# Scattering routed rows while projecting: one region per expert in place of gathers and accumulating scatters

## The reference, cut to what matters

```
proj = x @ w_in                       # 5 blocks of 512 columns
m    = concat(conv_mixer(proj), rg_lru(proj) * gelu(gate)) @ w_out
x    = layer_norm(ALPHA * x + m, ln1)
# routing: best of 4 groups, then the best 2 of its 4 experts
gates  = softmax(top-2 expert logits) * softmax(group logits)[group]
h = silu(x @ w1[e]) * (x @ w3[e])     # 16 experts, 1024 -> 256
y = sum over the row's 2 experts of (h * gate) @ w2[e]
out  = layer_norm(ALPHA * x + y, ln2)
```

## Time and profile before

| | us |
|---|---|
| median of three runs | 1322.22 (1317.29 to 1328.05) |
| profiled execution, first to last instruction | 1314.2 |
| TensorE busy in it | 1132.7 (86%) |
| VectorE busy | 710.5 (54%) |
| ScalarE busy | 522.3 (40%) |
| GpSimd busy | 298.0 (23%) |

### The profile page before, as it was taken

The page is one execution under the profiler, slowest core; times in us unless marked ns, Lnnn a source line. Parts: engine busy times, 40 slices in busy tenths (PEclk is TensorE's granted clock), DMA queues, the critical chain, the costliest instruction groups (busy, mean ns, idle before and its releaser), DMA issues. The chain is left out here.

```text
span 1314.2 us, 19578 instructions
## 1 busy us (share of the span) xinstructions
PE 1132.7 (86%) x5748; PEld 1021.3 (78%) x5749; DVE 710.5 (54%) x1131; ACT 522.3 (40%) x678; POOL 298.0 (23%) x254
## 2 busy tenths in 40 slices
PE   6999999999999999999999269999999899996000
PEld 6999999999999998888887157877787778885000
DVE  5676544644555564434334755555646445531698
ACT  4554533634445453333333204444445434421222
POOL 1000000000000021121211242345535443432244
PEclk9999999999999999999999559999999999999555
DMA  5422100200120155544432535787888877764822
GB/s 181 137 85 74 56 19 19 97 19 19 35 88 13 52 166 190 173 144 160 144 128 100 205 112 179 212 279 200 267 224 233 257 194 207 206 125 62 324 112 100
DMA packets 64423, 183.95 MB, mean 140 GB/s; under 512 B 7456, under 2 KB 34096, under 8 KB 60176
## 3 DMA queue, kind: packets, MB, share of 16 engines
q1 hardware_dynamic: 42464, 104.28, 22.4%
q0 software_dynamic: 17040, 61.57, 19.1%
q10 hardware_dynamic: 4896, 17.83, 3.3%
HBM read 125.70 MB, written 57.96 MB: 140 GB/s over the span
## 5 line engine op out<-in xcount | busy, mean ns | idle before, releaser
L1296 PE MATMUL ps_h<-w_hi,xt_hi 128*128 x336 | 136.5, 406 | 0.0
L1296 PE MATMUL ps_h<-w_hi,xt_lo 128*128 x336 | 132.8, 395 | 0.0
L1296 PE MATMUL ps_h<-w_lo,xt_hi 128*128 x336 | 132.8, 395 | 0.0
L272 PE MATMUL ps_vb_c<-x_hi,w_hi 128*128 (+1 forms) x320 | 114.0, 356 | 10.7 <-DVE x_lo L424 10.7
L272 PE MATMUL ps_vb_c<-x_lo,w_hi 128*128 (+1 forms) x320 | 113.2, 354 | 0.0
L272 PE MATMUL ps_vb_c<-x_hi,w_lo 128*128 (+1 forms) x320 | 113.1, 353 | 0.0
L272 PE MATMUL ps_va_b<-x_hi,w_hi 128*128 (+1 forms) x320 | 112.3, 351 | 0.0
L272 PE MATMUL ps_va_b<-x_hi,w_lo 128*128 (+1 forms) x320 | 112.1, 350 | 0.0
L272 PE MATMUL ps_va_b<-x_lo,w_hi 128*128 (+1 forms) x320 | 111.9, 350 | 0.0
L1246 POOL DMA_INDIRECT acc_scr<-out_sb,id_s x42 | 76.2, 1813 | 35.4 <-POOL id_s L1242 27.9
L193 POOL DMA_DIRECT2D w_raw<-in_w_in x15 | 8.0, 531 | 328.8 <-DVE w_lo L410 320.4
(11 more groups left out here) (246 smaller groups left out, 2722.3 us busy)
## 6 DMA issues: line engine op xcount, KB each, us to landing
w_raw<-in_w SPq DMA_DIRECT2D x16, 2048.0 KB, 8.6
w_raw<-in_w SPq DMA_DIRECT2D x16, 1024.0 KB, 9.2
w_raw<-in_w_in POOLq DMA_DIRECT2D x19, 512.0 KB, 3.7
w_hi_p<-in_x_rows SPq DMA_DIRECT2D x17, 512.0 KB, 3.8
x_scr<-w_lo_p ACTq DMA_DIRECT2D x17, 512.0 KB, 2.6
acc_scr<-w_lo_p ACTq DMA_DIRECT2D x17, 512.0 KB, 2.6
v<-acc_scr SPq DMA_DIRECT2D x17, 512.0 KB, 10.5
x_raw<-in_x_t SPq DMA_DIRECT2D x20, 416.0 KB, 3.5
```

The source lines that it names most:

```text
L272: mm = pe.matmul(ps[i][:, 0:CHUNK], w[:, i, k], x[:, k, bass.ds(c * CHUNK, CHUNK)], start=(k == 0 and n == 0), stop=(k == KT - 1 and n == 2))
L1296: mm = pe.matmul(ps_h[par][:], x[:, par, k], w[:, bass.ds(at, 1), k].rearrange("p o n -> p (o n)"), start=(k == 0 and n == 0), stop=(k == ...
```

## The change

`x1_scr` and `acc_scr` go. In their place are `xs_scr`, a region of CAP = 2080 rows for each of the 16 experts, `g_scr`, a gate for each of these rows, and `o_scr`, an output row for each slot of the 48 steps.

- **Zeroing.** After the first channel group of the mixer, SyncE writes zeros over the first 128 rows of each region, the gates of these, and the last 15 tiles of `o_scr` (`FEWEST` = 33 to 48), from a source 256 elements wide that is read four times.
- **Projection.** Row tiles lie in a ring of eight. The norm is two VectorE operations; the sum with beta on GpSimd and the stores of `x1` and ALPHA * `x1` go. TensorE's order is: six of the eight k-slices of tile t, transposes of t-1, a count for a pair of tiles, the last two k-slices, the router of t-1. For each pair of tiles VectorE routes (`assign`: groups, experts, one-hot; `places`: the row's place in its expert's region, with a running count), and GpSimd scatters each row tile twice into `xs_scr` and its gates twice into `g_scr`. The last two tiles (group `LAST`) are routed after the stage.
- **Before the experts.** `plan_steps` makes the list of steps: expert, first row in `xs_scr`, whether weights are split. `slots` turns places into rows of `o_scr` for the end. An expert's last tile begins early enough to be full (it overlaps the one before) where the expert has over 128 rows.
- **Experts.** SyncE loads the rows and the gates of step s+3 with plain transfers, after it has stored the output of step s-1, also plain. ScalarE keeps ALPHA/2 times the row tile, and VectorE adds it to the output when it leaves PSUM (`evict`, both halves). The weights are now loaded through GpSimd's queue.
- **Last stage.** GpSimd gathers each row's two output rows, VectorE adds them, and does the norm, gain and beta in two operations.

`assign` is 21 operations on 128 x 8 to 128 x 32 elements and `places` 14, nearly all of which wait for the one before; `free` in `load(s)` is s - 3.

The diff, cut to its core:

```diff
@@ mixer: mix_sync
         store_y(0, NCH - 1, True)
+        sp.wait_ge(s_zero, 1)
+        for e in range(NE):
+            sp.dma_start(xs_scr[e * CAP:e * CAP + P, :].rearrange("p (a d) -> p a d", d=ZC),
+                         zero.unsqueeze(1).broadcast_to((P, D // ZC, ZC))).then_inc(s_zo, 16)
+            sp.dma_start(g_scr[e * CAP:e * CAP + P, :], zero[:, 0:1]).then_inc(s_zo, 16)
+        for n in range(FEWEST, STEPS):
+            sp.dma_start(o_scr[n * P:n * P + P, :].rearrange("p (a d) -> p a d", d=ZC),
+                         zero.unsqueeze(1).broadcast_to((P, D // ZC, ZC))).then_inc(s_zo, 16)
         with sp.Fori(1, GROUPS - 1) as j:
             with sp.Fori(0, NCH - 1) as c:
                 store_y(j, c, False)
@@ class Router
+    def assign(self, dve, n):
...
+    def counts(self, pe, n, bank, before, ones):
+        pe.wait_ge(self.s_asg, n + 1)
...
+        pe.matmul(bank[:, 0:m * NE], before, rhs, start=True, stop=True)
+        pe.matmul(bank[:, 2 * NE:(2 + m) * NE], ones, rhs, start=True, stop=True).then_inc(self.s_cnt, 1)
+    def places(self, dve, n, bank):
...
+    def scatter(self, pool, n):
+        pool.wait_ge(self.s_sl, n + 1)
+        for t, rows, c in todo:
+            pool.indirect_dma_start(self.xs_scr, bass.IndirectOffsetOnAxis(self.sli[0:rows, t, c:c + 1], 0),
+                                    self.ring[t % NRING][0:rows], None).then_inc(self.s_sc[n % 4], 16)
+        pool.wait_ge(self.s_wts, n + 1)
+        for t, rows, c in todo:
+            pool.indirect_dma_start(self.g_scr, bass.IndirectOffsetOnAxis(self.sli[0:rows, t, c:c + 1], 0),
+                                    self.wts[0:rows, t, c:c + 1], None).then_inc(self.s_gs, 16)
@@ mix_project_phase: TensorE
+            for t in range(NT):
+                project(t, early)
+                if t >= 1:
+                    turn(t - 1)
+                for n in ends_at(t - 2):
+                    rt.counts(pe, n, ps_c, before, ones)
+                project(t, late)
+                if t >= 1:
+                    route(t - 1)
@@ mix_project_phase: VectorE, after residual, statistics and low half of y
+                dve.scalar_tensor_tensor(out=v, in0=v, scalar=mv[:, par, 0:1], in1=ln_g,
+                                         op0=ALU.subtract, op1=ALU.mult).then_inc(s_xn, 1)
...
+                dve.scalar_tensor_tensor(out=v, in0=v, scalar=rstd[:, par:par + 1], in1=ln_b,
+                                         op0=ALU.mult, op1=ALU.add).then_inc(s_x1, 1)
+                for n in ends_at(t - 2):
+                    rt.places(dve, n, ps_c)
+                if t >= 1:
+                    logits_out(t - 1)
+                for n in ends_at(t - 1):
+                    rt.assign(dve, n)
@@ moe_phase: SyncE
+            def load(s, par, h):
+                row = sp.value_load(plan[0:1, 1, bass.ds(s, 1)], min_val=0, max_val=NE * CAP - P)
...
+                if not early(s, 2):
+                    sp.wait_ge(s_xr, read)
+                    sp.wait_ge(s_tx, read)
+                    sp.wait_ge(s_g[par], there)
+                sp.dma_start(xg[:, par], xs_scr[bass.ds(row, P), :]).then_inc(s_xg[par], 16)
+                if not early(s, XS):
+                    sp.wait_ge(s_ev, free)
+                sp.dma_start(gate[:, slot(par, h)], g_scr[bass.ds(row, P), :]).then_inc(s_g[par], 16)
+            def store(s, par):
+                sp.wait_ge(s_ev, s + 1)
+                sp.dma_start(o_scr[bass.ds(s * P, P), :], out[:, par]).then_inc(s_st[par], 16)
+            def step(s, par, h, left):
+                if not early(s, 1):
+                    store(s - 1, 1 - par)
+                if left == 2:
+                    load(s + 3, 1 - par, h + 1 + par)
+            sp.wait_ge(s_plan, 1)
+            for n in range(LAST - 3, LAST + 1):
+                sp.wait_ge(rt.s_sc[n % 4], rt.landed(n))
+            sp.wait_ge(rt.s_gs, 16 * TOPK * NT)
@@ moe_phase: GpSimd
+            pool.dma_start(ew.w13_raw[:], w13[0]).then_inc(ew.s_r13, 16)
+            pool.dma_start(ew.w2_raw[:], w2[0]).then_inc(ew.s_r2, 16)
+            for n in (LAST - 1, LAST):
+                rt.scatter(pool, n)
...
+            with pool.Fori(2, NE) as e:
+                pool.wait_ge(s_13lo, e * 2)
+                pool.dma_start(ew.w13_raw[:], w13[bass.ds(e, 1)].rearrange("o p k n -> p (o k) n")).then_inc(ew.s_r13, 16)
+                pool.wait_ge(s_2lo, e)
+                pool.dma_start(ew.w2_raw[:], w2[bass.ds(e, 1)].rearrange("o p k n -> p (o k) n")).then_inc(ew.s_r2, 16)
@@ moe_phase: ScalarE, after x_hi(s + 1) and ahead of the weight split
+                act.activation(flat(xr[:, slot(par, h)]), xg[:, par], ACT.Copy, scale=ALPHA / 2).then_inc(s_xr, 1)
@@ moe_phase: VectorE, in place of the copy of half the output
+            def evict(s, par, h):
+                dve.wait_ge(s_o, s + 1)
+                dve.wait_ge(s_xr, s + 1)
...
+                for f in range(2):
+                    ins = dve.tensor_tensor(out[:, par, c], ps_o[f][:], flat(xr[:, slot(par, h), c]), ALU.add)
+                ins.then_inc(s_ev, 1)
@@ finish_phase: GpSimd
+            for t in range(NT):
+                for c, to in enumerate((v, v1)):
+                    pool.indirect_dma_start(to[0:n, t], None, o_scr,
+                                            bass.IndirectOffsetOnAxis(sfin[0:n, c, t:t + 1], 0)).then_inc(s_in[t], 16)
```

More of the change, by code:

```diff
@@ new lines, in landed, with mix_project_phase, sb, sem @@
+    def landed(self, n):
+        return 16 * TOPK * sum(GROUPED[i][1] for i in range(n % 4, n + 1, 4))
+def mix_project_phase(nc, x_t, w_in, w_lru, chan, y_scr, states, x_rows, w_out, w_router, ln, consts_in,
+                      xs_scr, g_scr, o_scr, logits, small, wreg, x_raw, rt):
+    with ExitStack() as ctx:
+        mx = mixer(nc, ctx, x_t, w_in, w_lru, w_out, chan, y_scr, states, x_rows, wreg, x_raw, xs_scr, g_scr, o_scr)
+        mix_sync, mix_gpsimd, mix_tensor, mix_scalar, mix_vector = mx.engines
+        STEPS_MIX = GROUPS * NCH
+        LAST = len(GROUPED) - 1
+        def sb(name, shape, dt=F32):
+            return ctx.enter_context(nc.sbuf_tensor(name, shape, dt))
+        def sem(name):
+            return ctx.enter_context(nc.semaphore(name))
+        squares, wr, ring = mx.squares, mx.wr, mx.ring
+        ident, before, ones = (squares[:, i] for i in range(3))
@@ L931, in lo2, with moe_phase @@
                           ALU.subtract).then_inc(self.s_2lo, 1)
-def route_phase(nc, consts, logits, ids, gates, plan, ew, w13, w2, ln, ln2, consts_in, small):
+def moe_phase(nc, rt, xs_scr, g_scr, o_scr, w13, w2, ln, consts_in, wreg, sfin):
     with ExitStack() as ctx:
@@ L1172, in experts_phase @@
+        xr, xg, out = rows(wreg[2], 0, XS), rows(wreg[3], 0, 2), rows(wreg[3], 2, 4)
+        gate = sb("gate", [P, XS])
+        consts = sb("consts_sb", [P, NCONST])
+        plan = sb("plan", [1, 3, STEPS + 2], I32)
         xt_hi = sb("xt_hi", [P, 2, KT, P], F32R)
@@ L1249, in step @@
-            def step(s, par, h, left):
-                if left == 2:
-                    gather(s + 3, 1 - par)
-                if not early(s, 1):
-                    add(s - 1, 1 - par)
-            for s in range(3):
-                gather(s, s % 2)
-            last = steps(pool, step)
-            add(last, 1)
-            pool.wait_ge(s_xg[0], last * 8 + 24)
-            pool.wait_ge(s_add, last * 16 + 16)
+            pool.dma_start(ew.w13_raw[:], w13[0]).then_inc(ew.s_r13, 16)
+            pool.dma_start(ew.w2_raw[:], w2[0]).then_inc(ew.s_r2, 16)
@@ L1304, in step @@
                 mm.then_inc(s_th, 1)
+            pe.wait_ge(s_con, 16)
+            rt.counts(pe, LAST, ps_c, consts[:, C_TRI:C_TRI + P], consts[:, C_ONE:C_ONE + P])
+            pe.wait_ge(s_vals, 1)
+            pe.wait_ge(rt.s_read, LAST + 1)
+            for i in range(3):
+                mm = pe.matmul(ps_c[0:1, 128 + i * (STEPS + 1):128 + (i + 1) * (STEPS + 1)], vals[:, i:i + 1],
+                               consts[:, C_ID:C_ID + STEPS + 1], start=True, stop=True)
+            mm.then_inc(s_pp, 1)
             turn(0, 0, 0)
-            last = steps(pe, step)
+            last, _ = steps(pe, step)
             output(last, pe.value_load(plan[0:1, 0, bass.ds(last, 1)], min_val=0, max_val=NE - 1))
@@ L1348, in step, with then @@
                 act.wait_ge(s_sil, s + 1)
+            rt.gate_exp(act, LAST)
+            ew.hi13(act, 0, first)
+            ew.hi2(act, 0, first)
             x_hi(0, 0)
-            last = steps(act, step)
+            residual(0, 0, 0)
+            last, _ = steps(act, step)
             h_hi(last)
-            out_half(last, 1)
         @block.vector
         def _(dve):
+            def then(ins):
+                rt.then(dve, ins)
             def h_lo(s):
@@ L1394, in _, with finish_phase @@
+            rt.assign(dve, LAST)
+            rt.places(dve, LAST, ps_c)
+            dve.wait_ge(s_con, 16)
+            plan_steps()
+            ew.lo13(dve, 0, first)
```

(8 more changed lines are left out.)

808 lines of the change are left out of this document (356 added, 452 removed).

## The result

The changed kernel takes 1502.6 us in the median of four runs (1499.8 to 1504.0), against 1323.9 (1317.3 to 1328.1, four runs, three of which were known ahead of the prediction) before: a ratio of 1.137, 95% interval 1.133 to 1.141. Forecast were 1339 us and a range of 1296 to 1363. The direction was the likeliest one of the forecast, the size was not in it. The profiled execution has a span of 1500.7 us; before it was 1314.2, so 186.5 us have to be found.

The account below looks back on a forecast made before the run. TensorE was taken to bound mixer, projection and expert steps, VectorE the routing tables and last stage. Terms +15 + 6 - 26 + 24.5 - 2 = +17.5 gave span 1331.7, median 1339.7, stated as 1339 us, range 1296 to 1363.

Parts of the forecast that it names:

- The direction: Whole kernel: slower than 1335 us, given 0.48, against 0.28 for faster than 1309 and 0.24 for within.
- Mixer, +15: Mixer: zeroing on SyncE's queue delays a y store, so TensorE idles 15 us once (9 to 25).
- Small columns that cost more: Mixer zeroing: 4-byte gate columns, named only as part of what could take the 15 us wait up to 25.
- Rival 5: Mixer: the zeroing does not hold it up, -15 us on any other case; no chance of its own.
- Projection, +6: Projection: count matmuls about 0.4 us a pair plus stalls, norm covered; together +6 us (0 to 16).
- The stall at the counts: Projection: TensorE waits 0 to 1 us for the pair's routing at the count matmuls, in eight pairs.
- To the experts, -26: Last projected tile to first expert matmul: 45 us instead of 71.1, saving 26 (20 to 31).
- Expert steps, +24.5: Expert steps: base 403.5 us, plus loads 3 us late in 14 steps, 42 us; 445.5 in all (-17.5 to +52.5).
- rival 3: Expert steps: weights go first, whole; loads 5 us late, 70 us, total 1367; 0.14, shared with forecast plus rival 4.
- Tail and last stage, -2: After the last expert matmul: tail gains 5.8 us, VectorE-bound last stage loses 3.9; -2 (-4 to +20).
- Rival 4: Last stage: GpSimd's gathers become the limit, 99 us instead of 89, +8 to +17; 0.14 with the forecast, shared with rival 3.

Follow-up runs that it names:

- e1: Changed kernel with the sixteen 4-byte gate columns of zeros written as one transfer of 16 rows of 512 bytes; 1420.7 us.
- e9: e8 with tile 16's y split moved behind the pair's routing on VectorE and the x1_t eviction on ScalarE; 1287.5 us, ratio to before 0.974.
- e8: Changed kernel plus e1, all zeroing spread over y stores, expert loads before stores, e6, tile 16's y split after tile 14's norm; 1295.3 us, ratio to before 0.978.
- e6: Changed kernel with the first two row loads not waiting for gate scatters, and expert 1's weights issued only after these loads land; 1493.7 us.
- e11: e9 with expert weights in six transfers of 4 KB per partition, and expert 0's weights on SyncE's queue; 1299.0 us, ratio to before 0.982.
- e4: Changed kernel with each expert's weights in six transfers of 4 KB per partition instead of two of 16 and 8 KB; 1435.9 us.

## Why the prediction was wrong, point by point

**Mixer, +15: measured +100.9. This step failed, in one term.** The row blocks were priced at 46 us and cost 44.5 (e1), TensorE's wait for them at 15 and was 15.9. "Small columns that cost more" had no term of their own in the sum, only a share of the 10 us up to the end of the range; beside the row blocks they cost 82. No row of before shows 4-byte writes side by side, so the bound was a guess, and it should have been much wider: sixteen transfers that nothing in the trace resembles stood ahead of a store that TensorE waits for. Rival 5 (-15) was wrong too.

**Projection, +6: measured +26.0.** Some 10 us of it is tile 14's round trip for the last tile's y (251.0 becomes 240.3 in e9, 10.0 of it in the pitch of the next tile; 8.7 are shown by the one move from e8 to e9). The order on VectorE there was in the code and I did not follow it. The rest, 15.3 us, is in e9 a pitch of 14.6 us in seven tiles with counts against 13.6 before, 5.2 us in the second tile, where the first norm is late, and 3.1 in the last; these were read, not tested. The stall at the counts came to 0 to 1 us as forecast, except at tile 14.

**To the experts, -26: measured -14.1.** All times here count from the end of the last tile's matmuls, 841.9 us. The plan was ready after 27.9 us (25.5 forecast), 2.5 of them before VectorE begins the last residual. The first load left after 41.2 where I had the last scatter landed at 32: the last row scatter was issued at 27, and such a scatter holds the load for 13 us (e6), not 2.5. It stands behind the 3 MB of expert 0's weights, for which the sum had no term; without them ahead of it the load follows after 3.8 us (e11). And GpSimd issues 3 MB for expert 1 just before that load, which then took 9.8 us to land where the sum left about 7. e6 gets back 9.9 us, 6.4 of it there; the late scatters stay.

**Expert steps, +24.5: measured +75.3.** This step failed too, in the size of one term. The mechanism was right, to the place: load behind store on SyncE, weights on the engines first. In the step shown the load is issued 2.1 us behind the weights and is wanted at 948.2. The lateness is 5.2 us, not 3. That is rival 3's value, but not its mechanism: the weights don't go through whole, they take turns with the smaller rows (e4). And behind each wait the clock falls, which costs about 2 us more; I had no term for that. So the late loads cost 96.7 us, 7.4 for each of 13, where I had 3 for each of 14, 42 in all. The base is lower than I said: with the loads in time the stage takes 399.5, not 403.5.

**Tail and last stage, -2: measured -1.5.** -3.8 and +2.3 for -5.8 and +3.9. Rival 4 did not come: the gathers of the last stage keep up.

With the columns and the late loads at their measured sizes the sum would have been 82 + 55 = 137 us higher, 1476; the rest is the projection and the start. Either of the two alone would have carried the sum beyond the upper end of 1363, and even with every term at the late end of its own range the sum is 1416. That the direction was right says little for the sum: it was given 0.48.

## What to carry to other kernels

A transfer's price is paid by whoever stands behind it: before putting transfers on a queue, list what follows them there and who waits for that, and take from the trace only prices of the same shape, words side by side above all. In a steady loop, issue the load whose buffer is already free ahead of the store that waits for this step's work; the order of two lines was worth 97 us. And where a wait is removed or moved, read the in-order engine behind it to the end, since the same round trip was first paid by the norm, then by the routing, and by nobody only in the third place.

## What the hardware showed that I had not expected

- Writes of 4 bytes to neighbouring words are slow (16 columns in 27.3 us) and hold up the larger writes that follow: fifteen 512 KB blocks took 42.2 us behind them, 21.4 without. The same words 512 bytes apart cost 3 us in all. Which distance is enough was not tried, nor whether the gate scatters, which also write 4-byte words, pay the same.
- The two kinds of write cost most when they alternate: 79 us over the row blocks' own 44, against 47 one after the other.
- After a wait of 5 us TensorE works on at a granted clock of 0.50: the eight transposes that take 1.04 to 1.09 us took 1.96 behind each of the thirteen late loads, and the granted clock of the stage was 0.91 instead of 0.99. Behind e4's waits of 1.6 to 2.3 us they took 1.09 us in twelve cases of thirteen, and the stage's clock was 0.99.
- Two queues on the same engines share them by packets and not by bytes: 190 packets of 3.7 KB beside 181 of 9.6 KB in 6 us.
